# Seven products for eight in two down projections, and first and last weight blocks in halves

## The reference, cut to what matters

```python
# first block
mod = silu(c) @ w_ada + b_ada                    # 1024 x 6144; its first 2048 columns: shift, scale
h = rms(x, norm_mix) * (1 + scale) + shift
proj = h @ w_in                                  # first columns: q 512, kv_lat 256, q_i 512, ...
...
gu = xb @ w_gu[e] + b_gu[e]                      # each expert: 1024 x 2048
g, u = gu[:, :1024], gu[:, 1024:]                # clipped; act = (u + 1) * g * sigmoid(1.702 g)
x = x + g_f * gate * (act @ w_dn[e] + b_dn[e])   # summed over each token's experts
# each of the two layers, second half
u = conv(rms(x, ffn_pre) @ w_up)                 # 2 x 2816 columns
hid = gelu(u[:, :2816]) * u[:, 2816:]
x = x + rms(hid @ w_down, ffn_post)              # w_down: 2816 x 1024
```

## Time and profile before

| | |
|---|---|
| median of 3 runs | 2075.01 us (2074.34 to 2078.17) |
| the profiled execution | 2079.1 us, span 2077.4 us, mean granted clock 0.988 |
| TensorE busy | 1974.8 us of the span, 95% |
| VectorE, ScalarE, GpSimd busy | 597.2, 409.3, 92.5 us |
| DMA | 582.20 MB, mean 280 GB/s |
| stages, from the span's start | front to about 355 us, experts to about 1288, first layer to about 1680, second layer to the end |

### The profile page before, as it was taken

One profiled execution on the slowest core, in us unless ns is written; L12 is line 12 of the kernel. 1 busy time (PEld: TensorE's weight loads), 2 busy tenths in 40 slices (PEclk: granted clock), 3 DMA queues, 4 the chain that ended last, 5 costly groups with the idle time before them and its releaser, 6 DMA issues.

```text
span 2077.4 us, 22981 instructions
## 1 busy us (share of the span) xinstructions
PE 1974.8 (95%) x9060; PEld 1137.3 (55%) x9060; DVE 597.2 (29%) x1240; ACT 409.3 (20%) x868; POOL 92.5 (4%) x167
## 2 busy tenths in 40 slices
PE   6999999999989899999898999999999999999998
PEld 2767885333333333333333334766888456778863
DVE  1387513122112112211121122542333035333311
ACT  2134213111111001111110112243222023422110
POOL 0000000000000000000000000200000011000000
PEclk9999999999999999999999999999999999999999
DMA  9655358999999999999999998153454334335430
GB/s 377 236 195 206 129 203 322 411 427 427 428 427 428 428 427 428 428 427 427 428 428 428 428 427 341 40 204 112 143 162 162 120 114 162 122 122 162 162 139 24
DMA packets 132852, 582.20 MB, mean 280 GB/s; under 512 B 9608, under 2 KB 55824, under 8 KB 106416
## 3 DMA queue, kind: packets, MB, share of 16 engines
q1 hardware_dynamic: 128240, 574.70, 69.5%
q0 software_dynamic: 4544, 6.57, 1.0%
HBM read 580.18 MB, written 2.63 MB: 281 GB/s over the span
## 4 chain that ended last, share of the span: by engine, by line
PE 74%; DMA 21%; DVE 3%; ACT 1%; issue 1%; SPq 0%; DVEq 0%; ACTq 0%
PE psum L357 52%; PE psum L675 11%; DMA work<-w_gu 11%; DMA ring<-w_gu 9%; PE psum L620 9%; PE psum L2118 1%; DVE work L1778 1%; PE psum L662 1%; DMA ring<-w_in 1%; PE psum L651 1%; DMA ring<-w_ada 0%; PE psum L1052 0%; ACT work L2439 0%; SPq L459 0%; DVE work L1776 0%
## 5 line engine op out<-in xcount | busy, mean ns | idle before, releaser
L357 PE MATMUL psum<-normed,ring 128*128 128x256 f32 (+1 forms) x2432 | 507.5, 370 | 0.2 <-PE psum L357 0.2
L357 PEld LDWEIGHTS psum<-normed,ring 128*128 128x128 f32 x2432 | 443.0, 191 | 60.8 <-issue 4.7
L620 PE MATMUL psum<-ring,normed 128*64 128x512 f32 x1024 | 234.5, 611 | 35.0 <-DMA ring<-w_gu 33.8
L620 PE MATMUL psum<-work,normed 128*64 128x512 f32 x1024 | 232.6, 608 | 33.1 <-DMA work<-w_gu 33.1
L357 PE MATMUL psum<-ring,work 128*128 128x512 f32 (+1 forms) x592 | 249.8, 581 | 0.1
L357 PE MATMUL psum<-work 128*128 128x128 f32 (+7 forms) x1152 | 185.1, 334 | 2.5 <-ACT work L2429 1.7
L357 PEld LDWEIGHTS psum<-ring,work 128*128 128x128 f32 x592 | 111.7, 190 | 130.6 <-issue 129.3
L620 PEld LDWEIGHTS psum<-ring,normed 128*64 128x64 f32 x1024 | 81.0, 141 | 186.3 <-issue 184.1
L620 PEld LDWEIGHTS psum<-work,normed 128*64 128x64 f32 x1024 | 80.5, 140 | 183.6 <-issue 183.6
L357 PEld LDWEIGHTS psum<-work 128*128 128x128 f32 (+2 forms) x1152 | 135.1, 186 | 65.0 <-issue 52.0
L357 PE MATMUL psum<-ring,normed 128*128 128x512 f32 (+2 forms) x400 | 160.5, 557 | 2.2 <-DMA ring<-w_in 1.8
(11 more groups left out here) (304 smaller groups left out, 1326.7 us busy)
## 6 DMA issues: line engine op xcount, KB each, us to landing
ring<-w_gu SPq DMA_DIRECT2D x64, 2048.0 KB, 27.4
work<-w_gu SPq DMA_DIRECT2D x64, 2048.0 KB, 27.5
work<-w_dn SPq DMA_DIRECT2D x32, 2048.0 KB, 27.4
ring<-w_dn SPq DMA_DIRECT2D x28, 2048.0 KB, 27.4
ring<-w_in SPq DMA_DIRECT2D x25, 2048.0 KB, 9.2
ring<-w_up SPq DMA_DIRECT2D x44, 1024.0 KB, 7.3
ring<-w_ada SPq DMA_DIRECT2D x11, 2048.0 KB, 9.4
ring<-w_down SPq DMA_DIRECT2D x10, 2048.0 KB, 7.8
```

The source lines that it names most:

```text
L357: return pe.matmul(out, lhsT, rhs, start=first, stop=last, **kw)
L620: ins = pe.matmul(b[r], self.hgT[:, 2 * q + k, r], ws[e][:, k, n0:n0 + 512], start=q == 0 and k == 0, stop=q == QUARTERS - 1 and k == 1, s ...
```

## The change

The order and grouping of loads and products change in three places, and the arithmetic in one.

1. **Front.** The first 2048 columns of w_ada are loaded by halves of the features: parts 0 and 1, each of two slots of 512 rows, each slot in four DMAs. w_in's first 1024 columns come as the slots "top" (rows 0 to 511) and "bottom" (rows 512 to 1023), each in two DMAs (q, then kv and qi). After part 0 the features 0 to 511 are formed and the products of q, kv and qi run over them; part 1's products and sums are interleaved with these. `ada(j)` no longer waits for its own result.
2. **Last w_gu quarter.** All pairs run it k outside, c inside, with a wait between the two k. In the very last pair its two slots are loaded as four halves: k = 0 of both experts, then k = 1 of both.
3. **Down projections.** The first 16 chunks are taken in 8 blocks of two. For a block, the four outputs of two token tiles by two column halves are made with seven products of sums instead of eight plain ones (Winograd's form of Strassen's scheme). GpSimd forms the token sums `s_sums`, VectorE the weight sums `t_sums` (two buffers; one sum is written over the weight in its slot). Four "sum" banks are joined by VectorE in `sevens_totals`; the last six chunks stay plain products, and each total is added to its bank before the norm. The next layer's transposes move to the middle of the last bank's six products.

```diff
-    s = [("ada", j) for j in range(4)]
-    s += [("win", 0), ("win", 1), ("win", 2), ("win", 3), ("ada", 4), ("wkv",), ("win", 4), ("ada", 5), ("win", 5)]
+    s = [("ada", 0), ("ada", 1), ("top",), ("ada", 2), ("ada", 3), ("bottom",)]
+    s += [("win", 2), ("win", 3), ("ada", 4), ("wkv",), ("win", 4), ("ada", 5), ("win", 5)]
...
+            if part == QUARTERS - 1:
+                sp.nop().then_inc(self.quarter_rest, 16)
...
+    def load_last_quarter(self, sp, io, S, slot, names, p):
+
+        for k in range(2):
+            for name in names:
+                part, e = name[2:]
+                src = io["w_gu"][bass.ds(2 * p + e, 1), part * 256:part * 256 + 256, :].rearrange("a (p k) n -> k p (a n)", p=P)
+                sp.dma_start(slot(S.no(name), 2, 2048)[:, k], src[k]).then_inc(*(S.fills(*name) if k == 0 else (self.quarter_rest, 16)))
...
+            if last and name[0:3] == ("gu", TWINS - 1, QUARTERS - 1):
+                if name[3] == 0:
+                    self.load_last_quarter(sp, io, S, slot, PAIR_SLOTS[i:i + 2], pair + name[1])
...
-                for c in range(4):
-                    for k in range(2):
+                for k in range(2):
+                    if k == 1:
+                        pe.wait_ge(self.quarter_rest, it * 32 * TWINS + 32 * (u + 1))
+                    for c in range(4):
                         ins = column(c, q, k, ws)
-                    ins.then_inc(*B.fills(*columns[c]))
+                        if k == 1:
+                            ins.then_inc(*B.fills(*columns[c]))
...
+            if kind == "ada" and j < 4:
+                if order.index(name) >= SLOTS:
+                    sp.wait_ge(*slot_used(order[order.index(name) - SLOTS]))
+                part, r0 = j // 2, 512 * (j % 2)
+                dst = slot(S.no(name), 4, 2 * 512).rearrange("p k (s n) -> p k s n", s=2)
+                src = io["w_ada"][r0:r0 + 512, 0:2 * D].rearrange("(k p) (s h n) -> h p k s n", p=P, s=2, h=2)[part]
+                for k in range(4):
+                    sp.dma_start(dst[:, k], src[:, k]).then_inc(*S.fills(*name))
...
+                sp.dma_start(dst[:, :, 0:512], src[:, :, 0:512]).then_inc(q_in[kind == "bottom"], 16)
+                sp.dma_start(dst[:, :, 512:], src[:, :, 512:]).then_inc(*S.fills(*name))
...
+            part, r = divmod(j, 2)
...
+            w = slot(S.no(("ada", j)), 8, 512)
+            if r == 0:
+                pe.wait_ge(*B.empty("a", part))
+            for k in range(4):
+                for s in range(2):
+                    g = 2 * (k % 2) + s
+                    ins = matmul(pe, bank("a", part)[32 * g:32 * g + 32], cond[:, 4 * r + k], w[:, 2 * k + s],
+                                 r == 0 and k < 2, r == 1 and k >= 2)
+            ins.then_inc(*(B.fills("a", part) if r else (ada_done, 1)))
...
             ins.then_inc(*B.fills("a", j))
-            pe.wait_ge(*B.ready("a", j))
-            pe.nop().then_inc(ada_done, 1)
...
-        for j in range(2):
-            ada_first(j)
-            first_transposes(j)
...
+                    pe.wait_ge(*B.empty("q", t))
+                for k in range(4):
+                    if t == 0:
+                        pe.wait_ge(h1_ready[k // 2], 2 * part + k % 2 + 1)
+                    ins = matmul(pe, bank("q", t), h[:, 4 * part + k, t * P:(t + 1) * P], w[:, k, 0:512], (part, k) == (0, 0), (part, k) == (1, 3))
...
+        first_transposes(0)
+        first_transposes(1)
+        ada_first(0)
+        first_transposes(2)
+        first_transposes(3)
+        ada_first(1)
+        sum_first(0)
+        q_part(0)
         ada_first(2)
-        first_transposes(2)
+        kv_part(0)
         ada_first(3)
-        pe.wait_ge(ada_done, 4)
-        pe.nop().then_inc(*B.fills("a", 0))
-        sum_first()
-        by_token(("q",), wait_slot("win", 0), 0, 512)
-        w = wait_slot("win", 1)
-        by_token(("kv",), w, 0, 256)
-        by_feature(("qi", 0), w, 256)
+        qi_part(0, 0)
+        sum_first(1)
+        qi_part(0, 1)
+        q_part(1)
+        kv_part(1)
+        for i in range(2):
+            qi_part(1, i)
...
+            for g in range(SEVENS // 4):
+                pool.wait_ge(hid_ready, l * FC + 8 * g + 8)
+                pairs = hid[:, 8 * g:8 * g + 8].rearrange("p (i k) t -> p i k t", k=2)
+                a11, a12, a21, a22 = (pairs[:, :, k, t * P:(t + 1) * P] for t in range(2) for k in range(2))
+                s1, s2, s3, s4 = (s_sums[:, i, 4 * g:4 * g + 4] for i in range(4))
+                step(pool.tensor_tensor(s1, a21, a22, ALU.add))
+                step(pool.tensor_tensor(s3, a11, a21, ALU.subtract))
+                step(pool.tensor_tensor(s2, s1, a11, ALU.subtract))
+                pool.tensor_tensor(s4, a12, s2, ALU.subtract).then_inc(s_ready, 1)
...
-            for d in range(4):
-                w = weights(d)
-                for k in range(4):
-                    if (d, k) == (0, 0):
-                        pe.wait_ge(hid_ready, l * FC + 16)
-                    for t in range(NT):
-                        for j in range(2):
-                            ins = product(t, j, 4 * d + k, w[:, k])
-                ins.then_inc(down_used, 1)
...
+            def seven(i, w):
+
+                a, b = 2 * i, 2 * i + 1
+                wa, wb = w[:, a % 4], w[:, b % 4]
+                last = i == SEVENS - 1
+
+                def product(name, lhsT, rhs, ends=False):
+                    if i == 0:
+                        empty(*name)
+                    return matmul(pe, bank(*name), lhsT, rhs, i == 0, ends and last)
+
+                def total(n, ins):
+                    if last:
+                        ins.then_inc(*B.fills("sum", l, n))
+
+                total(1, product(("sum", l, 1), tokens(a, 0), half(wa, 0), True))
+                product(("down", l, 0, 0), tokens(b, 0), half(wb, 0))
+                product(("down", l, 0, 1), s_sums[:, 3, i], half(wb, 1))
+                pe.wait_ge(t_ready, l * SEVENS + i + 1)
+                total(7, product(("sum", l, 7), s_sums[:, 2, i], half(wa, 1), True))
+                ins = product(("down", l, 1, 0), tokens(b, 1), t_sums[:, i % 2, 2])
+                if i % 2 == 1:
+                    ins.then_inc(down_used, 1)
+                total(5, product(("sum", l, 5), s_sums[:, 0, i], t_sums[:, i % 2, 0], True))
+                ins = product(("sum", l, 6), s_sums[:, 1, i], t_sums[:, i % 2, 1], True)
+                if last:
+                    total(6, ins)
+                else:
+                    ins.then_inc(t_used, 1)
+
+            pe.wait_ge(hid_ready, l * FC + 2 * SEVENS)
+            for i in range(SEVENS):
+                if i % 4 == 0:
+                    pe.wait_ge(s_ready, l * (SEVENS // 4) + i // 4 + 1)
+                if i % 2 == 0:
+                    w = weights(i // 2)
+                seven(i, w)
             pe.wait_ge(hid_ready, (l + 1) * FC)
-            ws = [weights(d) for d in range(4, DOWN_SLOTS)]
+            ws = [weights(d) for d in range(SEVENS // 2, DOWN_SLOTS)]
             for t in range(NT):
                 for j in range(2):
-                    if (t, j) == (1, 1) and l + 1 < LAYERS:
-                        norm_transposes(l + 1, 0, 0)
-                    for k in range(16, FC):
-                        ins = product(t, j, k, ws[k // 4 - 4][:, k % 4])
+                    if (t, j) == (1, 1):
+                        empty("down", l, 1, 1)
+                    for k in range(2 * SEVENS, FC):
+                        if (t, j, k) == (1, 1, FC - 3) and l + 1 < LAYERS:
+                            norm_transposes(l + 1, 0, 0)
+                        ins = matmul(pe, bank("down", l, t, j), tokens(k, t), half(ws[k // 4 - SEVENS // 2][:, k % 4], j),
+                                     (t, j, k) == (1, 1, 2 * SEVENS), k == FC - 1)
                     ins.then_inc(*B.fills("down", l, t, j))
             pe.wait_ge(*B.ready("down", l, 1, 1))
-            pe.nop().then_inc(down_used, DOWN_SLOTS - 4)
...
+            take(totals[:, 1], bank("sum", l, 1), "sum", l, 1)
...
+                if s == 1:
+                    total = totals[:, 1 + 2 * t + j]
+                    filled("down", l, t, j)
+                    take(TT(total, bank("down", l, t, j), total, ALU.add), "down", l, t, j)
+                    step(TT(half(xn[:, t], j), total, half(post[:, s], j), ALU.mult))
+                    continue
...
             for j in range(2):
-                take(STT(out=half(x[:, t], j), in0=half(xn[:, t], j), scalar=pr[:, n, 1:2], in1=half(x[:, t], j), op0=ALU.mult, op1=ALU.add),
-                     kinds[s], l, t, j)
+                ins = STT(out=half(x[:, t], j), in0=half(xn[:, t], j), scalar=pr[:, n, 1:2], in1=half(x[:, t], j), op0=ALU.mult, op1=ALU.add)
+                if s == 1:
+                    signal(ins, x_new, 4 * l + 2 * t + j + 1)
+                else:
+                    take(ins, "mix", l, t, j)
...
+            def weight_sums(i):
+
```

(28 more changed lines are left out.)

168 lines of the change are left out of this document (97 added, 71 removed).

## The result

The changed kernel takes 2053.64 us (median of 4 runs, 2051.9 to 2054.96) where the kernel before took 2074.7 on the same chip (median of 4; its first three gave the 2075.01 that the forecast starts from): a ratio of 0.9893, interval 0.9879 to 0.9907, or 21 us less. Measured once more it took 2053.92 against 2076.03, ratio 0.9885 (0.9869 to 0.9902). The forecast was 2050.4, with a range from 2046.5 to 2060.0. The sign and the mechanism were right; the gain is some 3 us smaller than forecast.

A forecast was written before the change was run, and what follows sets the result against it. Bounds differed by stage: DMA for the first weights and the experts, TensorE's instruction count at full clock from 1456 to 1680 us. The terms summed to -24.7 us, giving 2050.4 from the median 2075.01; range 2046.5 to 2060.

The forecast's parts named there:

- The down projection, -13.7: Both layers' down projections: 56 products replace 64, saving 6.86 us per layer, 13.7 us in two, with VectorE's sums hidden.
- the end of the chain, +0.25: Behind the last product: VectorE's add of bank to total comes before ScalarE's squares, costing 0.25 us.
- the passage, -1.0: Between the layers: TensorE's wait before the next layer's transposes goes whole as they move later, saving 1.0 us, once.
- The smallest slack: Start of the down projection: block 1's sums are ready 1.7 us before TensorE asks for them.
- The eight waits, -2.0: After later ada blocks: TensorE's eight waits for its own result go, saving 2.0 of 2.3 us.
- The front, -4.0: Kernel start: with loads reordered, q starts at 24.0 and qi ends at 58.0 instead of 62.0 us, saving 4.0.
- the slow-clock cost: Front, between q's start and qi's end: TensorE's lowered clock costs 1.8 us.
- the front would be held by its pieces: Rival, front: loads of 2 KB rows run below 300 GB/s, so gain 0 there and 2054.4 us; chance 0.12.
- The last quarter, -4.2: Last pair's last w_gu quarter: loading halves removes 2.7 us of wait and 1.5 of slow clock, saving 4.2 us.
- the 1.5 us of slow clock: Last w_gu quarter: the part of the -4.2 us from its 32 instructions no longer running at lowered clock.
- halves would land together: Rival, last w_gu quarter: first halves land with the second, its term is 0, total -20.5, 2054.6 us; chance 0.08.
- the rival on VectorE: Rival, down projection: slower subtractions make VectorE the bound and the kernel slower, gain eaten at 7.5 us a block; chance 0.02.

The follow-up runs named there:

- this part alone: Only the layers' part (seven products for eight, totals, later transposes) put on the kernel before, front and experts unchanged: 2063.5 us, ratio 0.993.
- the experiment: The changed kernel with the next layer's eight transposes back in front of the last bank's six plain products: 2052.31 us.
- 903.90 and 903.13 above: Two kernels: only the last w_gu quarter's change on the kernel before (2073.78 us), and the changed kernel with nine blocks instead of eight (2049.77 us).
- with 5.8: The changed kernel with each block's first subtraction made five times, eight subtractions a block on VectorE: 2059.72 us, ratio 0.9918.
- with 8.6: The changed kernel with each block's first subtraction made nine times, twelve subtractions a block on VectorE: 2105.12 us, ratio 1.0135.

## Why the prediction was right, and where its sizes were off

**The down projection, -13.7, the end of the chain, +0.25, and the passage, -1.0,** sum to -14.45; the stage measures -14.6, -14.1 with this part alone, and -14.5 between the means of all traces. The parts hold too: 32 rows of 128x512 fewer over both layers, each block 6.01 us, VectorE 2.9 us of it, and TensorE has no wait from block 0 to the last plain product. The smallest slack was forecast as 1.7 us at block 1; its sums end at 1980.1, and by the blocks' pace they are asked for at 1973.35 + 8.6 = 1981.9: 1.8. From VectorE's add of the last bank (2042.28) to the reciprocal (2044.15) it is 1.87, forecast 1.85. GpSimd's additions took 1.27 us each, estimated at 1.4. The passage is 1.26 by the experiment.

**The eight waits, -2.0:** 2.1 by the kernel with the nops put back. The reason stated was right that they show on the path, but the wait is the smaller part of each; the nop behind it, which the prediction didn't price apart, is the larger.

**The front, -4.0, was too large:** -2.9 between the two traces. Over all traces, the front's end lies at 68.74, 69.88 and 68.93 with the old front and between 64.98 and 66.86 with the new one (11 traces, mean 66.0): -3.2. It is 1.1 us short, and both halves of the sum have a part in it. The time up to q is 0.6 of it. To the end of the first 16 ada instructions the sum holds (18.57 us, forecast 18.5). For the eight transposes and 16 instructions behind them it left 2.5 us, to 21.0, though its own row has 1.92 for 16 such instructions at full clock; they took 2.95, to 21.52. The chain from there to q took 3.09, forecast 3.0: 24.61 instead of 24.0. From there to qi's end 34.0 was forecast and 34.5 measured, the slow-clock cost included (window clock 0.95 of 34.5 us: 1.7, forecast 1.8). That the front would be held by its pieces didn't happen: once q has started TensorE has no wait for a transfer, and between 17.1 and 38.1 us, the window that the rival named, DMA ran at 387 GB/s, where the rival needed less than 300.

**The last quarter, -4.2, was too large in this execution:** -2.8. The 2.69 of pause went, as forecast, and TensorE had no wait for w_dn behind it, which the prediction had called tight. Against the quarter loaded whole, with the same slowed quarter 2, it is only 1.0. The step that failed is the 1.5 us of slow clock. It was taken to hang on the second pause and to go with it; it came one quarter earlier, behind the first pause, in seven of the nine traces with the halves, and in the other two (903.90 and 903.13 above) the whole of it went, which gives 4.1 and 4.9. That halves would land together is refuted: the first halves let quarter 3 begin at 896.13 us from the experts' chain where the whole quarter let it begin at 899.13. The Trainium skill (DMA: Bandwidth & Descriptors, "Queues, rings and completion order") warns that the DMAs of one issuing engine needn't complete first-in first-out; here the two first pieces of 1 MB were usable at least 3.0 us ahead of the whole pieces of 2 MB, as the queue's order has it.

**The sum:** 22.3 by the trace against 24.7, made of 1.1 less in the front and 1.4 less in the quarter. From 2075.01 that gives 2052.7, and 2053.6 was measured. The break-even of the rival on VectorE was put at 7.5 us a block; with 5.8 the kernel is still 16 us faster than before and with 8.6 it is 29 slower, which a straight line puts at zero near 6.8 (an estimate; nothing was run between the two). The pauses cost more than their length: 2.31 us for 2.05 at full clock, and the lowered clock on top behind some of them.

## What to carry to other kernels

Seven products for eight pay where TensorE is busy at full clock and another engine stands: here VectorE has 3.1 us to spare in every 6.0, and the real limit was one block at the start. Price such a trade by the worst block and not by the mean, and count a pause of TensorE as longer than it is (2.31 us for 2.05 here, more where the clock falls behind it). When a pause is removed, ask what it used to hide: here the quarter at lowered clock ahead of it, which cost nothing while TensorE waited for a transfer anyway.

## What the runs showed that I had not expected

TensorE's lowered clock isn't only a matter of its pauses. In before's profiled execution it was at 1.2 GHz while TensorE was busy without a gap, in narrow products (windows of 2 us, columns as in the earlier trace rows):
```profile
245.00:247.00 2.00, 2.00 (x12) 2.00 (x11) 1.76 (x2) 0.00 (x0) 0.00 (x0) 0.50 1.05 321
247.00:249.00 2.00, 2.00 (x7) 1.75 (x8) 1.02 (x2) 0.00 (x0) 0.00 (x0) 0.50 0.91 331
```
The same products ran at 1.00 in the changed kernel. The Trainium skill (TensorE: Matmul & The Clock Gate, "What's actually happening") has half rate as the default that activity lifts; that agrees with the 0.50 behind the pause of 4.95 us, and these two rows, busy 2.00 of 2, don't show what set it there. Each such stretch costs 1.5 to 1.7 us (8.78 for 7.09); added up over windows of 5 us the profiled executions lose 14 to 20 us of TensorE's busy time to it, and 32 with twelve subtractions. Of these, 12 to 16 lie in the experts, where TensorE waits for weights anyway, so most of them cost the kernel nothing. It falls on other places in other executions of nearly the same kernel, and whether a pause of 2 to 3 us is followed by it differs too: of 19 pauses of 2.2 to 2.7 us ahead of 32 instructions in the experts of before, 9 were (8.4 to 8.8 us for the 32) and 10 were not (7.09). What decides that stays open. It is the likely reason (argued, not shown) why the medians scatter by 2 to 3 us; terms of 1 to 2 us could be read only in the traces, stage by stage.
